# Weight splits one unit earlier in the SSD groups and behind the boundaries, and a reordered first group, in a two-layer SSD / short-conv / ConvFFN trunk

## The reference, cut to what matters

```python
for i in range(DEPTH):                                   # 2
    h = rms_norm(x, mix_pre_g[i])
    m = ssd_mixer(h, ...) if i == 0 else shortconv_mixer(h, ...)
    x = x + rms_norm(m, mix_post_g[i])
    f = conv_ffn(rms_norm(x, ffn_pre_g[i]), ...)
    x = x + rms_norm(f, ffn_post_g[i])

def ssd_mixer(h, ...):
    zxbcdt = h @ w_in                                    # z | x, B, C | dt
    xbc = silu(causal_dwconv(xbc, conv_w, conv_b))       # 4 taps
    dt = softplus(dt_raw + dt_bias); a_head = -exp(a_log)
    y = ssd_scan(xs, dt, a_head, bs, cs) + xs * d_skip
    return rms_norm(y * silu(z), norm_w) @ w_out

def conv_ffn(h, ...):
    up = h @ w_up                                        # 2 * 2816 columns
    return (silu(causal_dwconv(up[:, :2816], conv_w, conv_b)) * up[:, 2816:]) @ w_down
```

## Time and profile before

| | us |
|---|---|
| time before, median of 3 runs (lowest to highest) | 1406.51 (1406.11 to 1406.72) |
| the profiled execution | 1405.03 |
| its span in the trace | 1403.3 |
| PE busy | 1364.0 |
| DVE busy | 787.1 |
| ACT busy | 568.7 |
| DMA, mean rate | 97 GB/s |

### The profile page before, as it was taken

The page is one execution under the profiler, slowest core; times in us unless marked ns, Lnnn a source line. Parts: engine busy times, 40 slices in busy tenths (PEclk is TensorE's granted clock), DMA queues, the critical chain, the costliest instruction groups (busy, mean ns, idle before and its releaser), DMA issues.

```text
span 1403.3 us, 15968 instructions
## 1 busy us (share of the span) xinstructions
PE 1364.0 (97%) x6494; PEld 1124.8 (80%) x6494; DVE 787.1 (56%) x1139; ACT 568.7 (41%) x874; POOL 24.3 (2%) x28
## 2 busy tenths in 40 slices
PE   8899999999799999999999999999999999999998
PEld 7677787777688978888888888888897888888886
DVE  4688877888622666565652246555456665564223
ACT  6565455665322644333332144322363333333112
POOL 0000000000000000000000000000000000000000
PEclk9999999999999999999999999999999999999999
DMA  4423333223232123333333322333313333333231
GB/s 120 123 86 105 105 106 113 83 91 105 91 120 90 46 78 111 98 91 104 91 119 106 105 60 76 105 91 120 106 45 106 105 93 103 91 91 134 90 105 60
DMA packets 181773, 135.70 MB, mean 97 GB/s; under 512 B 5645, under 2 KB 169893, under 8 KB 180677
## 3 DMA queue, kind: packets, MB, share of 16 engines
q1 hardware_dynamic: 181653, 134.62, 31.9%
q10 hardware_dynamic: 48, 0.07, 0.0%
HBM read 132.51 MB, written 2.16 MB: 96 GB/s over the span
## 4 chain that ended last, share of the span: by engine, by line
PE 86%; DVE 8%; ACT 2%; issue 2%; DMA 1%; DVEq 0%; SPq 0%; ACTq 0%
PE bank L825 18%; PE bank L826 18%; PE bank L827 18%; PE bank L886 9%; PE bank L887 9%; PE bank L888 9%; DVE mask L613 2%; PE bank L1002 1%; DVE feat L686 1%; DVE w_lo L562 1%; DVE feat L680 1%; PE bank L992 1%; PE bank L863 1%; DVE feat L684 1%; DVE decay L608 1%
## 5 line engine op out<-in xcount | busy, mean ns | idle before, releaser
L825 PE MATMUL bank<-h_hi,w_hi 128*128 128x512 f32 (+1 forms) x1352 | 517.8, 383 | 15.3 <-DVE w_lo L562 14.5
L827 PE MATMUL bank<-h_lo,w_hi 128*128 128x512 f32 (+1 forms) x1352 | 513.3, 380 | 0.0
L826 PE MATMUL bank<-h_hi,w_lo 128*128 128x512 f32 (+1 forms) x1352 | 513.3, 380 | 0.0
L562 DVE TENSOR_TENSOR w_lo<-w_raw,w_hi 128x1024 fp32r<-128x1024 f32 x228 | 278.4, 1223 | 347.6 <-ACT w_hi L345 347.6
L345 ACT ACTIVATE w_hi<-w_raw 128x1024 fp32r<-128x1024 f32 x228 | 238.5, 1052 | 210.0 <-PE bank L888 183.5
L825 PEld LDWEIGHTS bank<-h_hi,w_hi 128*128 128x128 f32 x1352 | 254.6, 188 | 70.1 <-ACT feat L397 14.0
L827 PEld LDWEIGHTS bank<-h_lo,w_hi 128*128 128x128 f32 x1352 | 254.4, 188 | 49.9
L826 PEld LDWEIGHTS bank<-h_hi,w_lo 128*128 128x128 f32 x1352 | 254.5, 188 | 48.0
L886 PE MATMUL bank<-w_hi,hid_hi 128*128 128x512 f32 x416 | 165.0, 397 | 0.0
L888 PE MATMUL bank<-w_hi,hid_lo 128*128 128x512 f32 x416 | 164.9, 396 | 0.0
L887 PE MATMUL bank<-w_lo,hid_hi 128*128 128x512 f32 x416 | 164.8, 396 | 0.0
(11 more groups left out here) (147 smaller groups left out, 971.6 us busy)
## 6 DMA issues: line engine op xcount, KB each, us to landing
w_raw<-in_ffn_w_up SPq DMA_DIRECT2D x88, 512.0 KB, 3.8
w_raw<-in_ssd_w_in SPq DMA_DIRECT2D x48, 512.0 KB, 3.9
w_raw<-in_ffn_w_down SPq DMA_DIRECT2D x44, 512.0 KB, 3.6
w_raw<-in_sc_w_in SPq DMA_DIRECT2D x24, 512.0 KB, 3.7
acs_b<-acs_dram SPq DMA_DIRECT2D x8, 1024.0 KB, 6.3
w_raw<-in_ssd_w_out SPq DMA_DIRECT2D x16, 512.0 KB, 3.6
w_raw<-in_sc_w_out SPq DMA_DIRECT2D x8, 512.0 KB, 3.5
x_tok<-in_x SPq DMA_DIRECT2D x4, 512.0 KB, 4.7
```

The source lines that it names most:

```text
L562: nc.vector.tensor_tensor(w_lo[slot(u)][:], w_raw[:, u % 2, :], w_hi[slot(u)][:].bitcast(F32), ALU.subtract).then_inc(w_lo_done, 1)
L825: nc.tensor.matmul(dst, wh, xh, start=start, stop=False)
L826: nc.tensor.matmul(dst, wl, xh, start=False, stop=False)
L827: return nc.tensor.matmul(dst, wh, xl, start=False, stop=stop)
```

## The change

It has four parts.

1. **Splits one unit ahead.** In the SSD groups all calls of `splits_to` (three places on ACT, four on DVE) ask for one unit more, and so does the call near the end of the three inner boundaries (`AHEAD + 2` for `AHEAD + 1`).
2. **First group on ACT.** For g = 0 only, `exps` comes after the silus of B and C and after `conv_in` of the first x tile, where it stood before all three.
3. **Start on PE.** `keep_warm` gives 4 matmuls twice where it gave 6 three times. The transposes of the parameter pages move from before unit 0 to behind its fourth k step and use bank 5; ACT copies them after the dt row. The cumulative sums (L955 and L958 before) move from before unit 1 to behind its third k step.
4. **First load of `acs_b`.** It follows the load of unit 4 in SP's queue, where it followed the load of unit 2.

```diff
@@ SP @@
-                    if u == GU * g + 2:
+                    if u == GU * g + (2 if g else 4):
                         if g == 0:
                             sp.wait_ge(acs_stored, 16)
@@ ACT @@
             splits_to(2)
+            act.wait_ge(dt_row_mm, 1)
+            nc.scalar.copy(dt_row[:], bank[7][0:HEADS, :]).then_inc(dt_row_done, 1)
             act.wait_ge(pages_turned, 1)
             for n in (0, 2, 3):
-                last = nc.scalar.copy(par[:, n, 0:ROWS[n]], bank[6][:, n * P:n * P + ROWS[n]])
+                last = nc.scalar.copy(par[:, n, 0:ROWS[n]], bank[5][:, n * P:n * P + ROWS[n]])
             last.then_inc(par_done, 1)
-            act.wait_ge(dt_row_mm, 1)
-            nc.scalar.copy(dt_row[:], bank[7][0:HEADS, :]).then_inc(dt_row_done, 1)
...
-                splits_to(GU * g + f + 3)
+                splits_to(GU * g + f + 4)
...
-                exps(g)
-                conv_in(g, 2, g * XG)
-                conv_out(g, 0)
-                conv_out(g, 1)
+                if g:
+                    exps(g)
+                    conv_in(g, 2, g * XG)
+                    conv_out(g, 0)
+                    conv_out(g, 1)
+                else:
+                    conv_out(g, 0)
+                    conv_out(g, 1)
+                    conv_in(g, 2, g * XG)
+                    exps(g)
                 conv_in(g, 3, g * XG + 1)
...
-                splits_to(GU * g + 4 + 3)
+                splits_to(GU * g + 4 + 4)
...
-                splits_to(GU * g + 5 + 3)
+                splits_to(GU * g + 5 + 4)
...
-                splits_to(b.end + AHEAD + 1)
+                splits_to(b.end + AHEAD + 2)
@@ DVE: the same four edits, and in addition @@
                     segments(g)
-                    splits_to(GU * g + 3)
+                    splits_to(GU * g + 4)
@@ PE @@
-                if c < C - 1:
-                    keep_warm(6, 7)
+                if c < C - 2:
+                    keep_warm(4, 7)
...
-            pe.wait_ge(params_landed, 16 * (N_PARAM - N_PAGE1))
-            pe.wait_ge(par1_done, 1)
-            for n in (0, 2, 3):
-                last = nc.tensor.transpose(bank[6][:, n * P:n * P + ROWS[n]], ...)
-            last.then_inc(pages_turned, 1)
...
-            pe.wait_ge(par_done, 1)
-            unit(0, bank[GROUP_BANKS[0]][:], behind={1: turn_dt})
-            pe.wait_ge(dt_vec, 3)
-            for c in range(C):
-                last = nc.tensor.matmul(bank[2][0:HEADS, c * P:(c + 1) * P], a_tok[...], tri[:], ...)
-            last.then_inc(acs_mm, 1)
-            nc.tensor.matmul(bank[3][:, 0:C * HEADS], tri[:], a_tok[:], ...).then_inc(acs_mm, 1)
-            unit(1, bank[GROUP_BANKS[1]][:])
+            def turn_pages():        # the same transposes, into bank 5, without the wait for par1_done
+            def turn_acs():          # the same two steps, with the wait for dt_vec
...
+            pe.wait_ge(par1_done, 1)
+            unit(0, bank[GROUP_BANKS[0]][:], behind={1: turn_dt, 3: turn_pages})
+            pe.wait_ge(dt_row_done, 1)
+            unit(1, bank[GROUP_BANKS[1]][:], behind={2: turn_acs})
```

More of the change, by code:

```diff
@@ L938, in _ @@
             last.then_inc(dt_row_mm, 1)
-            pe.wait_ge(params_landed, 16 * (N_PARAM - N_PAGE1))
-            pe.wait_ge(par1_done, 1)
-            for n in (0, 2, 3):
-                last = nc.tensor.transpose(bank[6][:, n * P:n * P + ROWS[n]], pages[0:ROWS[n], n, :], ident[0:ROWS[n], 0:ROWS[n]])
-            last.then_inc(pages_turned, 1)
             def turn_dt():
@@ L949, in turn_dt @@
                 last.then_inc(dt_mm, 1)
-            pe.wait_ge(par_done, 1)
-            unit(0, bank[GROUP_BANKS[0]][:], behind={1: turn_dt})
-            pe.wait_ge(dt_vec, 3)
-            for c in range(C):
-                last = nc.tensor.matmul(bank[2][0:HEADS, c * P:(c + 1) * P], a_tok[:, c * HEADS:(c + 1) * HEADS], tri[:],
-                                        start=True, stop=True)
-            last.then_inc(acs_mm, 1)
-            nc.tensor.matmul(bank[3][:, 0:C * HEADS], tri[:], a_tok[:], start=True, stop=True).then_inc(acs_mm, 1)
-            unit(1, bank[GROUP_BANKS[1]][:])
+            def turn_pages():
+                pe.wait_ge(params_landed, 16 * (N_PARAM - N_PAGE1))
+                for n in (0, 2, 3):
+                    last = nc.tensor.transpose(bank[5][:, n * P:n * P + ROWS[n]], pages[0:ROWS[n], n, :], ident[0:ROWS[n], 0:ROWS[n]])
+                last.then_inc(pages_turned, 1)
+            def turn_acs():
+                pe.wait_ge(dt_vec, 3)
+                for c in range(C):
+                    last = nc.tensor.matmul(bank[2][0:HEADS, c * P:(c + 1) * P], a_tok[:, c * HEADS:(c + 1) * HEADS], tri[:],
+                                            start=True, stop=True)
+                last.then_inc(acs_mm, 1)
+                nc.tensor.matmul(bank[3][:, 0:C * HEADS], tri[:], a_tok[:], start=True, stop=True).then_inc(acs_mm, 1)
+            pe.wait_ge(par1_done, 1)
+            unit(0, bank[GROUP_BANKS[0]][:], behind={1: turn_dt, 3: turn_pages})
+            pe.wait_ge(dt_row_done, 1)
+            unit(1, bank[GROUP_BANKS[1]][:], behind={2: turn_acs})
             for g in range(GROUPS):
```

## The result

| | before | after |
|---|---|---|
| time, median of 6 runs (lowest to highest) | 1405.61 (1404.61 to 1406.72) | 1379.72 (1379.59 to 1379.95) |
| ratio to before, 95% interval | | 0.9814 (0.9803 to 0.9824) |
| span of the profiled execution | 1403.3 | 1377.9 |
| PE busy | 1364.0 | 1356.2 |

The change takes 25.9 us off, 1.8%. The forecast was 1380.5, with 1375.5 to 1386 as its range. One execution of one kernel further down, silu_before_exps_everywhere, took 1676.72 us at a mean granted clock of 0.75; that kernel's median leaves it out.

What follows compares the result with a forecast made beforehand. TensorE was taken as the bound nearly everywhere, its work unchanged, so only its pauses could go. 1.4 + 9.35 + 3.8 + 11.4 = 26.0 us off gave 1379.0 for the profiled execution, 1380.5 for the median; range 1375.5 to 1386.

Steps and rivals of the forecast that it cites:

- 1a: SSD groups 1 to 7: low-part waits go, new silu waits of some 1.4 us at L974; gain 1.4 us.
- 1b: Output projection: unit 50's low part comes early; 7.75 us of waiting and 1.6 of half clock go, 9.35 us.
- 1c: Three boundaries: the fifth unit's wait goes and the sixth unit comes 2 us earlier; gain 3.8 us.
- (a): Start: ten warm-up matmuls removed, 2.24 us, all of it gained.
- (b) and (e): Start and first group: unit 0 not waiting for the pages' copy, 0.7 us; cumulative sums and unit 3's low part, 0.8.
- (c): First group: TensorE's wait of 6.4 us at L974 goes if the two silus come in time.
- (d): First group: TensorE's 3.34 us of busy time at clock 0.50 cost half, 1.7 us, which is gained.
- A: Rival: ScalarE's chain has unseen slack, so the group waits vanish, 12.5 us in place of 1.4; 1369.4 us, 7%.
- B: Rival: first group gives only 8 to 9 us, L985 waiting 2 to 3 for silus; 1383 to 1384, 15%.
- C: Rival: the clock falls at the start, where 10 of 28 warm-up matmuls are removed; 1383.9 us, 6%.
- D: Rival: a raw buffer or slot holds the splits, so only the first group gains; 1395 us, 3%.
- E: Rival: new 1.4 us waits at L974 make the clock fall; 1404.3 us, 1.5% no change, 1.5% slower.

Runs made afterwards that it cites:

- silu_before_exps_everywhere: The kernel after, with group 0's order (silus of B and C, third conv_in, then exponentials) in all groups; 1378.54 us.
- the first experiment: The kernel after, with the splits of groups 1 to 6 and the one at group 0's end back at their old places; 1386.33 us.
- the best kernel: The kernel after, with silus of B and C ahead of the third bank's conv_in in groups 1 to 7 and VectorE's low part behind xdd; 1367.49 us.

## Why the prediction was right, point by point

The parts measured one by one add up: 0.4 (groups), 9.4 (projection), 4.1 (boundaries), 8.2, 1.9 and 1.3 (first group and start) make 25.3 of the 25.9 us. The single executions behind these medians spread by up to 1.8 us, those of the kernel before by up to 2.7. The projection and the boundaries were added to the kernel before, the rest was taken out of the kernel after. The first load of `acs_b` (part 4) and the lead inside the first group were not run alone.

| term | predicted | traces | alone |
|---|---|---|---|
| 1a, seven groups | 1.4 | 0.5 to 0.7 | 0.4 |
| 1b, output projection | 9.35 | 9.3 | 9.4 |
| 1c, boundaries | 3.8 | 4.3 | 4.1 |
| 2 to 4, start and first group | 11.4 | 11.3 | 11.4 |

**The number.** It came closer than its parts. From the profiled execution the forecast was 1379.0, and the kernel after has 1379.67: the gain was put 0.7 too high. For the median 1.5 was added, since the profiled execution of the kernel before lay 1.5 under the median of the first three runs. In the kernel after the two are 0.05 apart (1379.67 and 1379.72). So 0.7 too low and 1.45 too high stand against each other in an error of 0.8, and that much is luck.

**1a.** The mechanism is as stated. The first silu of group 1 ended up where ScalarE's chain puts it, L984 came 0.23 earlier (predicted 0.22), and a new wait of 1.63 stands there (predicted some 1.4). The term was twice what it should have been all the same. The gain was counted at the start of L974 and carried over whole, as if nothing behind it changed: "Behind L974 nothing else is closer than 1 us". From L974 to the transposes of x it took 6.69 us before, and from L984 it takes 94.63 - 87.81 = 6.82 now. L984 is the one that waits now, and its eight matmuls take 1.00 us up to the next step (87.81 to 88.81) where in the first group, without a wait, they take 0.89 (45.17 to 46.06). That is 0.1 of the 0.23. The price of a restart is the term that was missing; the prediction named it as its lower bound of 0 and did not take it. The period of a group is 42.06, not just under 42.0.

**1b.** Right to a tenth, with both of its parts. One reading behind it was not exact: the clock did not fall "after the two long waits" but within them, at 51.8 with the wait until 55.26 and at 376.1 with the wait until 379.60. The cost was counted only over TensorE's busy time, so the term is not touched. The banks and the sums of squares that I named as next in line did not hold it.

**1c.** Mis-sized by 0.5. The term took the waits, and from start to start 1.5, 0.6 and 1.6. With the low parts made just in time there was a second cost: before, the first steps of the fifth unit and of the one behind it took 0.31 to 0.33 us (499.52, 504.86 and 505.17 behind the first boundary), now there is no such step behind 471.26. That is 0.08 + 0.10 + 0.08 over a step of 0.23: 0.26 behind the first boundary, where 1.5 were predicted and 1.77 gained.

**2 to 4.** 11.3 for 11.4, from pieces that were off both ways. (a) The start gave 1.79, not 2.24: the first `h_hi` went from 13.66 to 11.87, the line here, from ScalarE in the kernel after. Of the 0.45 that is missing, 0.30 is a wait for the pages to land, which the warm-ups had covered (in the list above); the sentence "all of it is gained" did not ask what stood behind them. The other 0.16 is the input: TensorE's first transposes of it start at 7.04 where it was 6.88. That wait (for `xn_tok`) was 0.4 before and is 0.6 here, and it lies between 0.4 and 1.2 in the other runs, at 1.1 with the warm-ups back, so it is not their doing. (b) and (e), the pages, the sums and unit 3, gave 1.75, not 1.5: the last matmul ahead of the product of C and B starts at 44.95 where it started at 48.49 in the kernel before, 3.54 earlier. (c) gave 6.55, not 6.4: that product stood 6.77 behind this matmul, and now 0.22. (d) less the new waits gave 1.19, not 1.3: from the product to unit 5 it took 9.21 and takes 8.02.

```profile
11.87 0.69 ACT L360 ACTIVATE h_hi<-bank,par 128x512 fp32r<-128x512 f32 x1 [1.54 <-PE bank L920]
```

In the walk, the masks were put at 42.9 to end and ended at 43.16, the large exponential at 43.1 (43.46), the silus of x done at 51.4 and 52.3 (51.83 and 52.73), unit 5 at 52.9 (53.19): 0.3 to 0.4 late throughout, and not 3. One step of the walk has the wrong cause: it lets the large exponential wait for the masks. They ended at 43.16, and the exponential stands right behind ScalarE's own table load (42.17 + 1.28 = 43.45), so ScalarE's own queue held it: the third bank's `conv_in`, which starts at 39.94 once TensorE has filled the bank, then a split and the load. The two chains end 0.3 apart, which is why the walk came out all the same. `acs_b` went out at 34.04 where I had 32.5: the store ahead of it, issued at 31.25, took 2.8 us to land, and not 1.66. It was still there before the masks wanted it. The new waits are 0.24 in sum, not 0.4.

**The table load.** In the first group, where the added load is, the split ahead of the silu's table load ends at 48.83 + 1.05 = 49.88 and the load starts at 49.91; it ends at 49.91 + 1.28 = 51.19, and the silu starts at 51.20. The Trainium skill (ScalarE: Activation LUTs, "What ACT_TABLE_LOAD costs") has a drain of about 1.38 us beside the load; no row here shows it, and the 2.8 us that it would have cost did not come.

**The rivals.** A (slack on ScalarE) is refuted by the new waits; its price, 1369.4, is close to what the kernel gives once ScalarE's chain is really shortened (1367.49). B had its mechanism, a wait for the silu of x, but at 0.24 us and not at 2 to 3. C fell with the warm-ups. D did not occur: no split in the groups waits for its load in the kernel after; that it can is shown by the first experiment, where a lead regained at once made ScalarE wait 4.00 us for a load. E did not occur: seven waits of 1.6 us left the clock at 1.00. The Trainium skill (TensorE: Matmul & The Clock Gate, "What's actually happening") has activity as what releases the throttle, which is why C had a place. These runs agree in so far as every low stretch ahead of the end, in all the kernels here, began in an idle time of TensorE of 3.83 us or more, and none in one of 1.64.

What the prediction missed altogether is the worth of the lead. It read the lead as a wait exchanged for a wait, which is right for this kernel, and did not ask what the lead makes possible: 12 us more by one reordering on ScalarE and one on VectorE.

## What to carry to other kernels

When a wait is removed, follow the consumer to its next wait and read the chain behind that one; if the chain has no idle time in it, only the slack between the two is gained. Then shorten that chain: a lead that gains nothing can be the precondition for an order that does, so try the two together and not only each alone. A helper that works one unit ahead should not stand between two steps that somebody waits for (here VectorE's low part between the masks and `xdd`), and where a lead is to begin or end, change it by one unit at a time where its load has already landed.

## What the runs showed of the hardware

- The granted clock fell to 0.50 around idle times of TensorE of 6.39, 7.58, 6.76 and also of 3.83 us, each time for 6.8 us, and each time it had fallen before the wait ended: at 51.8 with the wait until 55.26, at 376.1 until 379.60, at 49.7 until 51.95 and at 344.2 until 344.75. It came back 3.4, 3.3, 4.6 and 6.2 us after TensorE had gone on. Seven idle times of 1.6 us in one kernel left it at 1.00, and so did removing 10 of 28 warm-up matmuls.
- A wait costs more than its length. Eight short matmuls take 1.00 us behind one and 0.89 without, and behind the first large matmul after a wait the next starts 0.31 us later instead of 0.23. The same 0.31 also stands without a wait, where a large matmul follows transposes (46.31 and 46.62 in the kernel after). Over seven waits that is up to 1 us: the best kernel gained 12.2 where the waits it removed summed to 11.4.
- The store of the cumulative sums took 2.8 us to land in the kernel after, where a weight load had been issued 0.2 us ahead of it, and 1.66 in the kernel before; that it is the load that slows it was not tried.
